# One program of two transformer blocks: mLSTM norm joined with memory attention, two later norms joined, memory keys kept on chip, delta gates at the end, a new order in the experts and in the mLSTM scan

## What is computed

```python
def memory_attention(q, mem_k, mem_v):              # 4 heads of 64, 256 memory rows
    p = softmax(einsum('bshd,bmhd->bhsm', q * 64**-0.5, mem_k))
    return einsum('bhsm,bmhd->bshd', p, mem_v)

def step(carry, inp):                               # mLSTM, one chunk of 128 tokens, 4 heads, 2 directions
    C, n, m = carry; qb, kb, vb, ib, fb = inp
    b = cumsum(fb)
    d = where(causal, b[..., :, None] - b[..., None, :] + ib[..., None, :], -inf)
    m_t = maximum(max(d, -1), b + m)
    s = (qb @ kb.T) * exp(d - m_t)
    num = s @ vb + exp(b + m - m_t) * (qb @ C)
    h = num / maximum(abs(den), exp(-m_t))          # den: the same with n in place of C
    w_s = b_last - b + ib
    m_new = maximum(b_last + m, max(w_s))
    C_new = exp(b_last + m - m_new) * C + (exp(w_s - m_new) * kb).T @ vb

y  = (norm_per_head(h_f + h_b) * norm_g + skip * xc) * silu(z)      # behind the mLSTM
hb = silu(xb @ w_gate[e]) * (xb @ w_up[e]); yb = hb @ w_down[e]     # one expert, 1024 -> 512 -> 1024
y_dn = rms_norm(o_f + o_b, dn_norm) * silu(dn_gate)                 # behind the delta rule
y_rk = (norm_per_head(wkv_f + wkv_b) * ln_w + ln_b + bonus) * silu(rk_gate)
g = -exp(a_log) * softplus(ab + dt_bias); beta = sigmoid(ab)        # the delta rule's gates
```

## Time and profile before

| | us |
|---|---|
| three runs | 6880.01, 6883.26 (median), 6884.94 |
| the profiled execution, its own time | 6885.65 |
| its span in the trace | 6883.4 |
| TensorE busy in the span | 5539.8 (80%) |
| VectorE, ScalarE, GpSimd busy | 2341.4 (34%), 1146.1 (17%), 302.0 (4%) |

### The profile page before, as it was taken

One profiled execution on the slowest core, in us unless ns is written; L12 is line 12 of the kernel. 1 busy time (PEld: TensorE's weight loads), 2 busy tenths in 40 slices (PEclk: granted clock), 3 DMA queues, 4 the chain that ended last, 5 costly groups with the idle time before them and its releaser, 6 DMA issues. The chain is left out here.

```text
span 6883.4 us, 94918 instructions
## 1 busy us (share of the span) xinstructions
PE 5539.8 (80%) x39018; PEld 3019.6 (44%) x39018; DVE 2341.4 (34%) x3942; ACT 1146.1 (17%) x1846; POOL 302.0 (4%) x320
## 2 busy tenths in 40 slices
PE   7998868894986557789779989898468998867778
PEld 4554433333356535233244338888434443322243
DVE  2334310003205654000054465555542220433331
ACT  1223100001210020000032122111101111422111
POOL 0000000001010000000000000000000000211100
PEclk9999869996998777899879999999789999989989
DMA  2110255553133330755422242223221222467721
GB/s 104 36 36 31 87 202 206 201 217 115 50 110 104 108 128 26 287 187 188 163 89 83 75 148 58 64 60 69 79 96 40 68 69 87 154 236 257 244 104 64
DMA packets 554582, 813.66 MB, mean 118 GB/s; under 512 B 171448, under 2 KB 302904, under 8 KB 553720
## 3 DMA queue, kind: packets, MB, share of 16 engines
q1 hardware_dynamic: 486072, 629.12, 27.4%
q0 software_dynamic: 28544, 103.82, 4.2%
q10 hardware_dynamic: 39616, 75.51, 3.0%
HBM read 967.61 MB, written 209.19 MB: 171 GB/s over the span
## 5 line engine op out<-in xcount | busy, mean ns | idle before, releaser
L672 PE MATMUL op_acc<-op_w,op_m 128*128 128x512 f32 x1024 | 452.1, 602 | 61.9 <-DMA op_w<-in_w_out 61.9
L158 PE MATMUL hi_acc<-xT,hi_w 128*128 128x512 f32 x1024 | 446.1, 595 | 7.7 <-DMA hi_w<-in_odd_w_in 7.7
L672 PEld LDWEIGHTS op_acc<-op_w,op_m 128*128 128x128 f32 x1024 | 196.4, 194 | 303.8 <-issue 240.8
L158 PEld LDWEIGHTS hi_acc<-xT,hi_w 128*128 128x128 f32 x1024 | 193.5, 191 | 242.6 <-issue 234.4
L158 PE MATMUL ri_acc<-xT,ri_w 128*128 128x512 f32 (+1 forms) x576 | 257.6, 607 | 10.7 <-DMA ri_w<-in_even_w_in 10.7
L508 PE MATMUL na_acc<-xT,na_w 128*128 128x512 f32 x448 | 221.2, 642 | 41.0 <-DMA na_w<-in_na_w_in 35.0
L158 PE MATMUL di_acc<-xT,di_w 128*128 128x512 f32 x512 | 224.7, 597 | 0.0
L158 PE MATMUL mi_acc<-xT,mi_w 128*96 128x512 f32 (+1 forms) x512 | 223.9, 597 | 0.0
L3518 PE MATMUL le_gp<-le_g,xT 128*128 128x512 f32 x512 | 220.9, 592 | 0.0
L1154 PE MATMUL moe1e_g_ps<-moe1e_wg,moe1e_xb 128*64 128x512 f32 x768 | 178.3, 619 | 30.9 <-DMA moe1e_wu<-in_exp_w_up 23.9
L1239 DVE TENSOR_SCALAR moe0e_y<-moe0e_y_ps,moe_weight 128x512 f32<-128x512 f32 x48 | 36.0, 750 | 461.6 <-DMA scratch_y_rows<-moe0e_y 444.9
(11 more groups left out here) (660 smaller groups left out, 8784.3 us busy)
## 6 DMA issues: line engine op xcount, KB each, us to landing
moe0e_wg<-in_exp_w_gate SPq DMA_DIRECT2D x48, 2048.0 KB
moe0e_wu<-in_exp_w_up SPq DMA_DIRECT2D x48, 2048.0 KB
moe0e_wd<-in_exp_w_down SPq DMA_DIRECT2D x48, 2048.0 KB
moe1e_wg<-in_exp_w_gate SPq DMA_DIRECT2D x48, 2048.0 KB
moe1e_wu<-in_exp_w_up SPq DMA_DIRECT2D x48, 2048.0 KB
moe1e_wd<-in_exp_w_down SPq DMA_DIRECT2D x48, 2048.0 KB
op_m<-scratch_mixedT SPq DMA_DIRECT2D x32, 512.0 KB, 8.5
op_w<-in_w_out SPq DMA_DIRECT2D x32, 512.0 KB, 9.3
```

The costliest lines, as they stand in the source:

```text
L158: mm = pe.matmul(self.acc[i % 2][0:n, h * BANK:(h + 1) * BANK], self.wbuf[i % 3][:, k, 0:n], self.rhs[:, k, h * BANK:(h + 1) * BANK], star ...
L672: mm = pe.matmul(acc[:, n % AHEAD, h * BANK:(h + 1) * BANK], m[:, k, n * P:(n + 1) * P], wb[:, k, h * BANK:(h + 1) * BANK], start=(k == 0) ...
```

## The change

- `memory_keys` writes to tiles that stay on chip (and still to HBM); the neighbourhood stage leaves its memory queries in such a tile; ma0 loads nothing and stores its output in two halves.
- The steps of memory attention become a class, `MemorySteps`, with one method per engine and step. ma1 is gone: `mlstm_out` (mln) runs these steps between the pieces of the mLSTM norm, with one buffer (`sets` = 1) for transposes and for read-outs in PSUM, four of eight tiles normed by ScalarE, `skip * xc` by ScalarE, and scale and skip as one VectorE operation.
- dnn and rkn become `even_out` (evo): both sums per tile, the variances by wide operations over all heads, fused scale, bonus and gate, all gates loaded at once.
- Experts: the order of TensorE, separate semaphores for gate and up, loads in the order gate, up, down over both lanes, two tiles of y, the second of which is also h.
- Scan: the eight chunks written out, inputs double, the stabilizers of all chunks ahead of the loop, the next chunk's rows, maxima, differences and exponentials between the units, its scores ahead of the state updates, one of two products' scalings on ScalarE.
- Delta gates: made behind the third gate projection, their chain at the end.

The diff, cut to its core:

```diff
+class MemorySteps:
+    def tensor(self, pe, n):
+        if n < self.N:
+            pe.wait_ge(self.exps, max(n - 1, 0))
...
+        if 0 <= n - 2 < self.N:
+            k = n - 2
+            pe.wait_ge(self.probs, k + 1)
+            pe.wait_ge(self.probs_T, max(k + 1 - self.sets, 0))
...
+        if 0 <= n - 3 < self.N:
+            k = n - 3
+            pe.wait_ge(self.probs_T, k + 1)
+            pe.wait_ge(self.kept, max(k + 1 - self.sets, 0))
...
+    def vector(self, dve, n, link):
...
+        if n >= 4:
+            self.take(dve, n - 4)
-                def load_in(b, e, **only):
-                    sp.dma_start(wg[b][:], w_gate.rearrange("e (k p) f -> e p k f", p=P)[e], **only).then_inc(in_loaded[b], 16)
-                    sp.dma_start(wu[b][:], w_up.rearrange("e (k p) f -> e p k f", p=P)[e], **only).then_inc(in_loaded[b], 16)
+                def load_in(which, experts, new):
+                    for w, source, loaded in ((wg, w_gate, gate_loaded), (wu, w_up, up_loaded)):
+                        for l, b in enumerate(which):
+                            only = {} if new is None else {"cond": new[l]}
+                            sp.dma_start(w[b][:], source.rearrange("e (k p) f -> e p k f", p=P)[experts[l]], **only).then_inc(loaded[b], 16)
+                for load in (load_in, load_down):
+                    for c in range(2):
+                        load(streams(c), begin[c], None)
+                next_in(0, None, 0)
+                next_in(0, None, 1)
+                next_down(0, None, 0)
+                with sp.Fori(0, TURNS - 2) as i:
+                    next_in(1, i, 0)
+                    next_down(0, i, 1)
+                    next_in(1, i, 1)
+                    next_down(1, i, 0)
                         hide(first, i, c)
-                        if more:
-                            turn_x(*following, 0)
+                        for part in range(2):
+                            if more:
+                                turn_x(*following, part)
+                            if c == 1 or first > 0:
+                                down(*before, part)
                         turn_hidden(first, i, c)
-                        if more:
-                            turn_x(*following, 1)
-                        down(first, i, c)
@@ experts, ScalarE @@
-                        if some:
-                            store(*before, 0)
+                        if more:
+                            keep_x(*following, 0)
                         act.wait_ge(gates, count(first, i, 2, c + 1))
                         act.wait_ge(h_turned, count(first, i, 2, c))
-                        act.activation(h[:], g_ps[:], ACT.Silu).then_inc(gated, 1)
+                        if first:
+                            act.wait_ge(y_stored[1], count(first, i, 32, 16 * c - 16))
+                        act.activation(h, g_ps[:], ACT.Silu).then_inc(gated, 1)
                         if more:
-                            keep_x(*following, 0)
+                            keep_x(*following, 1)
...
-                        if some:
-                            store(*before, 1)
+                        if c == 1 or first > 0:
+                            store(*before)
@@ experts, VectorE @@
+                    for q in range(H):
+                        dve.wait_ge(y_stored[q], count(first, i, 32, 16 * c))
+                        if q == 1:
+                            dve.wait_ge(h_turned, count(*later, 2, more + 1))
+                        dve.tensor_scalar(y[q], y_ps[:, c, q * BANK:(q + 1) * BANK], column(weight, c, first, i), None,
+                                          ALU.mult).then_inc(y_kept, 1)
@@ scan, TensorE @@
+                for t in range(NC):
+                    more = t + 1 < NC
+                    for u in range(2):
+                        number(t, u)
+                    if more:
+                        rows_of_a(t + 1)
+                    for u in range(2, 5):
+                        number(t, u)
+                    if more:
+                        rows_of_M(t + 1)
+                    for u in range(5, U):
+                        number(t, u)
+                    if more:
+                        score(t + 1)
+                    for u in range(U):
+                        update(t, u)
@@ scan, VectorE @@
+                for t in range(NC):
+                    add(t, 0)
+                    add(t, 1)
+                    if more:
+                        maxima_of(t + 1)
+                    for u in range(2, 5):
+                        add(t, u)
+                    if more:
+                        differences(t + 1)
+                    for u in range(5, U):
+                        add(t, u)
...
+                    if more:
+                        weigh(t + 1)
...
+                    if more:
+                        weigh_values(t + 1)
@@ mlstm_out, the order of all engines @@
+        ORDER = [("token", n) for n in range(3)]
+        for n in range(3, NT):
+            ORDER += [("token", n), ("memory", n - 3)]
+        ORDER += [("root", 0)]
+        for n in range(NT - BY_ACT):
+            ORDER += [("norm", n), ("memory", NT - 3 + n)]
+        first = NT - 3 + NT - BY_ACT
+        for i in range(NI):
+            ORDER += [("row", i), ("memory", first + i)]
+        ORDER += [("memory", n) for n in range(first + NI, steps.N + 3)]
@@ even_out, VectorE, per tile @@
+                    dve.tensor_tensor(da[:, n, :], da[:, n, :], db[:, n % 4, :], ALU.add).then_inc(summed, 1)
+                    link(dve.tensor_tensor(ra[:, n, :], ra[:, n, :], rb[:, n % 4, :], ALU.add))
+                    link(dve.tensor_reduce(sums[:, n % 2, :], rv, AX, ALU.add))
+                    dve.scalar_tensor_tensor(out=rv, in0=spread(sums[:, n % 2, :], RD), scalar=-1.0 / RD, in1=rv, op0=ALU.mult,
+                                             op1=ALU.add).then_inc(centred, 1)
+                    if n >= 1:
+                        spreads(n - 1)
@@ delta_inputs, TensorE @@
-                pe.wait_ge(ab_loaded, 16)
-                ...
-                mm.then_inc(ab_made, 1)
-                for i in range(N + 2):
+                for i in range(N + 1):
                     if i < N:
                         rows.multiply(pe, i)
-                    if i == 0:
+                    if i == NI + 2:
+                        small_gates()
+                    if i == N:
+                        pe.wait_ge(turned_used, NI - HEADS)
                         pe.wait_ge(g3, 1)
```

More of the change, by code:

```diff
@@ new lines, in coming, with next_in @@
+                def coming(table, b, most, first, i):
+                    later = table[0:1, b * TURNS + first + 1:(b + 1) * TURNS].rearrange("p (t a) -> p t a", a=1)
+                    return sp.value_load(later[:, 0 if i is None else i, :], min_val=0, max_val=most)
+                def next_in(first, i, c):
+                    experts = [coming(expert, b, E - 1, first, i) for b in streams(c)]
+                    new = [coming(fresh, b, 1, first, i) for b in streams(c)]
+                    sp.wait_ge(ups, count(first, i, 2, c + 1))
+                    load_in(streams(c), experts, new)
@@ new lines, in next_down @@
+                def next_down(first, i, c):
+                    experts = [coming(expert, b, E - 1, first, i) for b in streams(c)]
+                    new = [coming(fresh, b, 1, first, i) for b in streams(c)]
+                    sp.wait_ge(results, count(first, i, 2, c + 1))
+                    load_down(streams(c), experts, new)
+                begin = [[sp.value_load(expert[0:1, b * TURNS:b * TURNS + 1], min_val=0, max_val=E - 1) for b in streams(c)] for c in range(2)]
+                for load in (load_in, load_down):
+                    for c in range(2):
+                        load(streams(c), begin[c], None)
@@ L1191, in _ @@
                 all_turns(pe, turn)
+                for part in range(2):
+                    down(TURNS - 1, None, 1, part)
             @block.scalar
@@ new lines, in update @@
+                def update(t, u):
+                    d, h = units[u]
+                    b = u % 2
+                    if u == 0:
+                        pe.wait_ge(vw_ready, t + 1)
+                    pe.wait_ge(states_used, max(t * U + u - 1, 0))
+                    for j in range(2):
+                        mm = pe.matmul(sp_[0:QC, b, j * V:(j + 1) * V], kts[t % 2][:, d, (2 * h + j) * QC:(2 * h + j + 1) * QC],
+                                       vw[:, u, :], start=True, stop=True)
+                    mm.then_inc(states, 1)
@@ L1695, in _ @@
+                for part in range(2):
+                    steps.store(sp, mem_rows, part, mem_stored)
+                sp.wait_ge(mem_stored, 32)
             @block.gpsimd
@@ L1712, in _, with add_skip @@
[L1712 to L1714 removed]
+                def add_skip(i):
+                    if i < NI:
+                        act.wait_ge(ex_loaded[i % 3], 16 * (i // 3 + 1))
```

(1 more changed line is left out.)

948 lines of the change are left out of this document (561 added, 387 removed).

## The result

| | before | after |
|---|---|---|
| median of the runs, us | 6882.32 | 6615.0 (6608.11 to 6622.97) |
| ratio, 95% interval | | 0.9612 [0.9595, 0.9629] |
| the profiled execution, its span, us | 6883.4 | 6606.1 |
| mean granted TensorE clock | 0.889 | 0.904 |

What follows compares the result with a forecast made beforehand. Stages stand in a row with barriers, so each is paid in full. Terms of -165, -87, -17, -51, -7 and 0 sum to -327 from 6885.65, less 2.4: 6556 us; range 6475 to 6665, forecast alone 6500 to 6615.

Steps and rivals of the forecast that it cites:

- the experts: Both expert stages together: 165 us less, bounds 95 and 200.
- later norms: The two later norms: 90 us against 141.30, 51 less, bounds 43 and 58.
- Experts, a step without a stall: Expert stages: a step without a stall falls from 23.20 to 22.35 us, 20 us less per stage.
- Experts, the stalls: Expert stages: TensorE's stalls for h, 57 and 36 us, go except for 15 us per stage, bounds 0 and 60.
- pair of stores: Rival, chance 0.14: the experts' two y stores run one after the other, some 120 us given back, 6676 us.
- Experts, the clock: Expert stages: TensorE's low-clock time in and behind stalls goes, 16 us in the first stage, 12 in the second.
- Experts, start and end: Expert stages: earlier first products gain 8 us, the end 2; the second stage also loses later up-weight waits.
- Scan: mLSTM scan: a chunk falls from 38.2 to 26.5 us, stage 238 against 325.30, 87 less, bounds 43 and 100.
- scan stays chained: Rival, chance 0.17: the mLSTM scan takes 32 us a chunk, 44 us more than forecast, 6600 us in all.
- mLSTM norm: mLSTM norm joined with second memory attention: 131 to 133 us against 149.80, 17 less, bounds 0 and 32.
- First memory attention and delta inputs: First memory attention 7 us less, needing no loads; delta inputs 0, bounds -13 and +5.
- Slower than before: Rival, chance 0.02: the two y stores need over 28 us in every expert step; 7060 us at 34 a pair.

Runs made afterwards that it cites:

- The experiment: Changed kernel with each y store of the experts issued as two, one per stream, rows outermost: 6514.74 us, ratio 0.9473 to the kernel before.
- one edited statement: Kernel before, with only its y stores in the experts issued as two, one per stream, rows outermost: 6721.36 us, ratio 0.9778.

## Why the forecast was right in part

Two terms fell outside their own bounds, in opposite directions: the experts gave 92 us (bounds 95 to 200) and the later norms 65 (43 to 58).

**Experts, a step without a stall.** Forecast 22.35 us, measured 22.81, so 9 us a stage (24 x 0.39) where 20 stood. The step that failed is the 6.87 us put down for every group of 32 matmuls. That is the distance from the gate to the up product only. One behind which transposes come lasts 6.97 (1137.48 - 1130.51), and the split down product has two such ends, 3.59 + 3.59. The transposes and the hidden waits came out as said.

**Experts, the stalls.** Slack right (20.3 us), remaining stalls mis-sized: forecast 15 us a stage, measured 27.3 and 32.9. In the second stage that leaves nearly all of them: of the 36 us of stalls before, 21 were to go and 2.6 did (42.0 - 32.9 - 6.5). The step that failed is the weighing of 17 us for a loaded pair side by side against 24 to 34 for one after the other. The two stores share their bandwidth; the pairs that held up TensorE took 20.3 us and the stall behind them from issue to landing, 30.2 at most (20.3 + 9.9). The argument taken from the earlier trace rows had this in it, 33 GB/s on a quiet queue, and the rule was cited beside it; the forecast nevertheless took the price of the better reading. The rival *pair of stores* put 60 us a stage on it where 12 and 18 more than forecast came, since only eight and six pairs were slow enough and a stall is 3 to 5 us long. (Its own terms, 12 steps x 7 us x 2 stages less 30, give 138 and not 120.) Kind right, price too high.

**Experts, the clock.** 16 and 12 us were to go with the stalls; 4 and 10 did. Slow product groups cost 20.7 us in the first stage before and 17.1 after (each group's time above the usual one of its kind, summed). With the stalls still there, their slow restarts stay. The experiment bears it out: without the stalls they are 6.7 us. The tie is not one to one, though: in the second stage 10 of the 12 us went while the stalls stayed, in fewer and longer waits. This term should have hung on the number of stalls and not have stood beside them.

**Experts, start and end.** The first gate product comes 18.3 us after the stage begins for 27.6, and the 6.9 us wait ahead of the second one is gone (by the code for weights; the profile names no releaser), while up and down products now wait 4.8: 11 us in all (9.3 + 6.9 - 4.8) for a forecast of 8. The end gained 1.4 of the 2 forecast, for the last stores still share their bandwidth; spread, it gains 10.6 more (18.5 to 7.9 us from the last down product to the end). Sum for the first stage: 9 + 30 + 4 + 11 + 1 = 55 against 52.7 measured and 90 forecast. For the second, where the start gave 18 of 17 forecast, it is 9 + 3 + 10 + 18 + 1 = 41 against 39.6 measured and 75 forecast.

**Scan.** 238 forecast, 237.7 measured. Chunks are 2097.24 - 2070.12 = 27.1 us apart; the forecast had 26.5. The parts fit less well than the sum, and that they meet to 0.3 us is luck: units and rows take 15.2 us for 13.5, scores 3.6 for 3.6, updates 8.4 for 8.5, so eight chunks take 5 us more than forecast, and what stands ahead and behind takes 5 less (21 for 26):

```profile
2070.12 0.49 PE L1616 MATMUL ms_n<-ms_v,ms_wt 128*128 128x193 f32 x2
...
2085.32 3.73 PE L1605 MATMUL ms_c<-ms_q,ms_k 96*128 96x128 f32 x32
2088.89 1.47 PE L1628 MATMUL ms_s<-ms_vw,ms_kt 128*96 128x193 f32 x8
...
2097.24 0.49 PE L1616 MATMUL ms_n<-ms_v,ms_wt 128*128 128x193 f32 x2
```

The rival *scan stays chained* (32 us a chunk, each handover slower and the clock as before) did not come about: the granted clock rose from 0.82 to 0.91. Even with the interleaving taken out three chunks take 2137.56 - 2045.33 us, 30.7 each.

**mLSTM norm.** The row stall was seen rightly and nearly sized: 26 us forecast, 22.9 measured. VectorE's own work was put too high (88 for 80.8). The step that failed is "about 5 us to the first sum": that holds for the first tile alone (4.1), and the third and fourth wait 10.1 and 5.2 more behind 3 MB of gates and the memory's queries in the queue. The forecast had looked at the start and not at what is queued between the tiles.

**Later norms.** 90 forecast, 76.6 measured. VectorE's work was right within 2 us (55.9 for 58). The margins behind the start (5.6 for 5) were too wide: between the phases 0.6 us and not 5, at the end 6.7 and not 12, waits in the rows 7.0 and not 10. Stores set the pace only at times:

```profile
4751.84 1.28 DVE L2079 SCALAR_TENSOR_TENSOR evo_o<-evo_tp,evo_par,evo_ga 128x1024 f32<-128x1024 f32 x1 [1.60 <-PE evo_tp L2096]
4753.53 1.28 DVE L2079 SCALAR_TENSOR_TENSOR evo_o<-evo_tp,evo_par,evo_ga 128x1024 f32<-128x1024 f32 x1 [0.40 <-DMA scratch_mixedT<-evo_o]
```

Of the 7.0 us, 5.0 are waits for transposes (the mean granted clock of the stage is 0.54), and 2.0 are waits for stores.

**First memory attention and delta inputs.** -8.4 for -7 and -0.5 for 0. In the delta inputs both halves of the argument hold: the small products take 23.76 us (forecast 24) because the clock falls under them, and the product behind pays 16.33 for 13.9.

**Rivals and range.** *Pair of stores* was the true mechanism at about a third of its price: of its 120 us, 30 came as stalls and 14 as slow products that stayed. *Slower than before* wanted over 28 us for the pair in every step, and only the slowest came to 30. (Its sum for 34 us a pair is wrong by its own terms: 24 steps of 37.7 us in each stage give some 7165 and not 7060.) The forecast's own range (6500 to 6615) just holds the median, and that it does is luck: the experts fell 73 us short, and 14 us from the later norms and 16 from stages that the change does not touch made up for a part. The wider range (6475 to 6665) holds it without them.

## What to carry to other kernels

Before hiding a wait for a DMA behind a second buffer, divide its bytes by its time on a quiet queue: a store at a fraction of the stage's rate is slow by its shape, and one edited statement gave 150 us in the two expert stages, where the new order, the new loads and the second tile gave 92. Terms that live on one another (a stall and the slow products behind it) belong in one term of the sum; in the first stage they failed together. And when one engine alternates between two chains of work, put the piece that another engine waits for next ahead of the piece whose own wait is open; that moved 18 of 142 us without a buffer.

## What the runs showed of the hardware

Small products at full clock: the first 4.6 us of the block of 512 products of 8 columns ran at 29.2 ns each, and the rest at 53.3 ns, after the granted clock had fallen from 1.00 to 0.50 (2.4 to 1.2 GHz) at 3542.8, though the engine issued without a pause. Pieces of 64 to 128 of them between wide products ran at 29.2 ns as well, except that the clock fell under one of five.

Load lengthens a store by about the same factor whatever its shape, and so costs the slow shape more microseconds. From quiet to the slowest under load a single store of 256 KB with an outermost dimension of two went from 6.3 to 15 us (2.4 times) and one with the rows outermost from 1.4 to 3.9 (2.8 times); a pair went from 11.6 to 28 us against 2.7 to 5.7.
